# Retention with its norm taken token by token and turned afterwards, and its heads' work placed between projection units

## The chip, the cores and the metric

The kernel runs on one NeuronCore of one Trainium2 chip. The metric is the device time of one execution in microseconds (us).

## The reference, cut to what matters

The network has two conditioned transformer layers, then two post-normed ones; the first of those holds the retention that is changed here. There are 256 tokens and 1024 features.

```python
# x: (B, T, D) = (1, 256, 1024);  H = 4 heads, dk = 256, dv = 512, chunks of C = 128 tokens
proj = x @ w_in                                   # w_in: 1024 x 6144
q, k, v, gate = jnp.split(proj, [1024, 2048, 4096], axis=-1)
q = _rope(q);  k = _rope(k) * dk ** -0.5
def body(state, inp):                             # one chunk of tokens, all heads
    s = einsum('bhid,bhjd->bhij', qi, ki) * intra # decay gamma^(i-j) for i >= j, else 0
    inner = einsum('bhij,bhje->bhie', s, vi)
    cross = einsum('bhid,bhde->bhie', qi * xi, state)
    state = gamma_c * state + einsum('bhjd,bhje->bhde', ki * zeta, vi)
    return state, inner + cross
mu  = mean(y, axis=-1);  var = mean((y - mu) ** 2, axis=-1)     # over the 512 of a head, per token
y   = (y - mu) * rsqrt(var + 1e-5)
mix = (silu(gate) * y) @ w_out                    # w_out: 2048 x 1024
```

With two chunks the recurrence is the same as one causal 256 x 256 score matrix with decay, and both kernels compute it so. After it come `x = layer_norm(alpha * x + mix)` and a SwiGLU.

## The kernel before, in words

**Layout and precision.** Activations lie with features on partitions and tokens along the free dimension (`[128, feature block, 256 tokens]`). Every weight product is done in three fast passes on fp32r operands: each operand is split into a high part (a copy in fp32r) and a low part (the rest), and `product3` (L260) issues hi*hi, hi*lo and lo*hi. Other products (scores, outputs, norms) are plain fp32 matmuls, each of which appears in the trace as two passes. A transpose appears as one.

**Units.** Weights stream in units of 1024 rows x 256 columns (1 MB) through four raw buffers. SyncE issues the DMA of a unit once the unit four before it has been split. `act_split` copies the raw unit to its high part on ScalarE, `dve_split` subtracts on VectorE for the low part; there are three split buffers, so unit n+3 is split only when PE has finished unit n. Both functions look two units ahead of the one they are called for. `pe_pair` does a unit's two blocks of 128 columns (48 matmuls of 256 columns), `project_rows` the same for the values, with tokens on the output's partitions.

**Order.** There is no scheduler: each engine runs its instructions in the order in which its own function writes them, and semaphores count them. `Engine.bank` gives out the eight PSUM banks in rotation and lets PE wait for the consumer of the tile that held the bank eight allocations ago.

**Retention** (`Retention`, L1608; `pe_retention`, `act_retention`, `dve_retention`, `pool_retention`):
- eight units of q and k, each 128-block of which is copied to `rt_raw` by ScalarE and rotated (a product with `rt_rot` on PE, GpSimd and VectorE elementwise);
- eight units of v, two units a head, copied from PSUM to `rt_v` by VectorE;
- eight units of the gate, two units a head, through Silu to `rt_g` on ScalarE;
- then the heads' block, a loop over six steps in which scores run for head i, outputs for head i-1, and mean and norm for head i-2. `pe_ret_scores` gives 128 x 384 scores, VectorE multiplies the decay in (`rt_S`, two buffers). `pe_ret_outputs` gives y with features on partitions, in four blocks of 128 for a head. The mean over features is a product with ones, centred by VectorE; squares by ScalarE, summed by 16 passes with one column (`pe_ret_norm`); the root is on ScalarE, the reciprocal and a diagonal matrix on VectorE, and its product with ones spreads 1/std over the partitions. VectorE multiplies it in, GpSimd multiplies the gate by y (`rt_g`), ScalarE and VectorE split the result into `rt_hi` and `rt_lo`.

`pe_deep_out` then multiplies by `w_out` in eight units: for each 256 output columns one over heads 0 and 1, one over heads 2 and 3. `act_layer_norm` and its partners follow, with a root on ScalarE. The input of the retention is the final norm's result, split by `act_program` and `dve_program` into `k.x`.

Of the kernel before, what the change touches and what calls it, by code (L numbers as in the profile page):

```python
# [1606 lines left out]

class Retention:  # L1608
    def __init__(self, k):
# [13 lines left out]
        self.dst = [(self.q if m < 8 else self.k)[:, m % 8, :] for m in range(16)]  # L1623


RET_COLS = [256 * c for c in range(8)]

# [10 lines left out]
def pe_retention(e, x):  # L1638
    k, w = e.k, e.k.io["ret_w_in"]
    t = Retention(k)  # L1640
    k.after(4, sp_retention)
# [9 lines left out]
    for c in range(8):  # L1651
# [5 lines left out]
        if c == 0:  # L1657
            pe_rope(e, t, "ret", 14, ("raw", "ret", 14))
            pe_rope(e, t, "ret", 15, ("raw", "ret", 15))
    for c in range(8):  # L1660
        u = take(e, ("ret_g", c), w, 0, KC, 4096 + 256 * c, 256)
        pe_pair(e, u, x, T, [("ret_g", 2 * c + j) for j in range(2)], [(k.scalar, ("ret_g", 2 * c + j)) for j in range(2)])
    for i in range(RET_HEADS + 2):
        if i < RET_HEADS:
            pe_ret_scores(e, t, i)
        if i >= 2:
            hd = i - 2
            bank = e.bank(("ret_mean", hd), k.scalar, ("ret_mean", hd))
            for c in range(4):
                e.wait_ge(k.scalar, ("ret_y", hd, c))  # L1670
                mm = e.matmul(bank[:, 0:T], k.ones[:, :], t.y[:, hd % 2, c, :], c == 0, c == 3)
            mm.then_inc(k.product, ("ret_mean", hd))
        if 1 <= i <= RET_HEADS:
            pe_ret_outputs(e, t, i - 1)
        if i >= 2:
            pe_ret_norm(e, t, i - 2)
# [13 lines left out]
def pe_ret_outputs(e, t, hd):  # L1690
    k, s = e.k, hd % 2
    e.wait_ge(k.vector, ("ret_S", hd))
    e.wait_ge(k.vector, ("ret_v", 7, 1))
    for c in range(4):
        e0 = hd * RET_DV + c * P
        bank = e.bank(("ret_o", hd, c), k.scalar, ("ret_y", hd, c))
        e.matmul(bank[:, 0:T], t.v[:, 0, e0:e0 + P], t.S[:, s, 0:T], True, False, loose=True)
        e.matmul(bank[:, P:T], t.v[:, 1, e0:e0 + P], t.S[:, s, T:384], False, True, loose=True).then_inc(
            k.product, ("ret_o", hd, c))


def pe_ret_norm(e, t, hd):
    k = e.k
    bank = e.bank(("ret_stat", hd), k.scalar, ("std", ("ret", hd)))
    e.wait_ge(k.scalar, ("ret_sq", hd, 3))
    for tb in range(TB):
        for c in range(4):
            mm = e.matmul(bank[:, tb:tb + 1], t.sq[:, c, tb * P:(tb + 1) * P], k.ones[:, 0:1], c == 0, c == 3)
    mm.then_inc(k.product, ("ret_stat", hd))
    rows = e.bank(("ret_rows", hd), k.vector, ("ret_normed", hd, 3))  # L1710
    pe_rows(e, TB, [rows[:, tb * P:(tb + 1) * P] for tb in range(TB)])


def act_retention(e):
# [9 lines left out]

    over_tiles(e, "ret", RET_COLS, act_split, lambda i, name: raw(i), lambda e: None)
# [8 lines left out]
    e.wait_ge(k.product, ("ret_g", 15))  # L1734
    for i in range(RET_HEADS + 2):
        if i >= 2:
            hd = i - 2
            e.wait_ge(k.product, ("ret_mean", hd))
            if hd:
                e.wait_ge(k.vector, ("ret_centred", hd - 1, 3))  # L1740
# [684 lines left out]
```

## Time and profile before

| | |
|---|---|
| time, median of 3 runs | 3046.66 us |
| lowest and highest | 3038.80, 3049.42 us |
| the profiled execution's own time | 3043.53 us |
| its span | 3041.7 us |
| TensorE (PE) busy | 2876.0 us, 95% |
| VectorE (DVE) busy | 1336.7 us, 44% |
| ScalarE (ACT) busy | 1022.7 us, 34% |
| GpSimd (POOL) busy | 149.8 us, 5% |
| DMA | 406.20 MB |

How to read it: the span runs from the first to the last instruction of one execution, and the time is a little longer. All times in the views are us from the span's start, durations of single instructions are in us in a timeline and in ns as means. PEld is PE's loading of the stationary operand, which overlaps its matmuls. A matmul's own duration holds its way through the array, so the pace of a row of them is read from start to start. L96 is the helper that issues all matmuls, L99 transposes, L103 and L104 activations (without and with an accumulated sum), L107 two-tensor operations of VectorE and GpSimd. The granted clock of PE is given as a share of full speed, 1.00 for 2.4 GHz and 0.50 for 1.2 GHz.

### The profile page before, as it was taken

To read this page: it belongs to the slowest core of one execution; us is meant where nothing else is said; L and a number is where in the kernel's file an instruction comes from. 1 tells how busy PE (TensorE), PEld (TensorE's weight loads), DVE (VectorE), ACT (ScalarE), POOL (GpSimd) and SP (SyncE) were. 2 spreads that over 40 slices of the span, in tenths; PEclk is the share of its full clock that TensorE was granted. 3 is DMA by queue.
4 is the path that set the end of the run, shared out by engine and by line. 5 is a ranking of instruction groups with operands and counts; after the bars stand their busy time and mean duration, and the time that the engine had idled before them with its cause. 6 is when DMAs were issued, how large, how long until landed. Compare 5 with 4: busy or idle time off the path is not lost.

```text
span 3041.7 us, 41711 instructions
## 1 busy us (share of the span) xinstructions
PE 2876.0 (95%) x18212; PEld 2535.8 (83%) x18212; DVE 1336.7 (44%) x1813; ACT 1022.7 (34%) x1322; POOL 149.8 (5%) x166
## 2 busy tenths in 40 slices
PE   6999999799999999999989799999889989999898
PEld 4878778588787877877878589999889989989898
DVE  3323242364433234323354555564455543546554
ACT  3222232332321223222242443444344444323443
POOL 1000010000000000000011000010110010000100
PEclk9999999968999999999999899999899999959999
DMA  7434354501434434344333045555145545544452
GB/s 236 153 113 152 117 168 130 162 1 51 130 118 146 143 128 146 125 139 146 114 116 127 15 139 181 167 174 186 61 145 187 168 153 183 168 52 93 138 194 80
DMA packets 398181, 406.20 MB, mean 134 GB/s; under 512 B 7216, under 2 KB 397056, under 8 KB 397872
## 3 DMA queue, kind: packets, MB, share of 16 engines
q1 hardware_dynamic: 398000, 403.53, 42.3%
q8 instruction: 145, 2.38, 0.3%
q14 instruction: 36, 0.29, 0.0%
HBM read 402.38 MB, written 1.12 MB: 133 GB/s over the span
## 4 chain that ended last, share of the span: by engine, by line
PE 87%; DVE 6%; ACT 4%; DMA 1%; issue 1%; POOL 1%; SPq 0%; POOLq 0%; ACTq 0%; DVEq 0%
PE bank L96 86%; DVE w_lo L107 1%; PE bank L99 1%; ACT w_hi L103 1%; DVE tmp L115 1%; ACT x_hi L103 1%; POOL acc L107 1%; ACT df_e L104 1%; DVE x_lo L115 0%; DMA w_raw<-in_ffn_w_in 0%; DVE df_e L115 0%; ACT sq L103 0%; DMA w_raw<-in_mix_w_out 0%; DMA hT<-in_hT 0%; DVE df_sc L124 0%
## 5 line engine op out<-in xcount | busy, mean ns | idle before, releaser
L107 DVE TENSOR_TENSOR w_lo<-w_raw,w_hi 128x2048 fp32r<-128x2048 f32 (+2 forms) x331 | 693.4, 2098 | 951.2 <-ACT w_hi L103 951.1
L96 PE MATMUL bank<-x_hi,w_hi 128*128 128x256 f32 (+1 forms) x3128 | 1037.1, 332 | 42.9 <-DVE x_lo L115 25.9
L96 PE MATMUL bank<-x_lo,w_hi 128*128 128x256 f32 (+1 forms) x3128 | 1029.6, 329 | 0.0
L96 PE MATMUL bank<-x_hi,w_lo 128*128 128x256 f32 (+1 forms) x3128 | 1028.7, 329 | 0.0
L103 ACT ACTIVATE w_hi<-w_raw 128x2048 fp32r<-128x2048 f32 (+2 forms) x331 | 578.7, 1751 | 588.8 <-PE bank L96 272.2
L96 PEld LDWEIGHTS bank<-x_hi,w_hi 128*128 128x128 f32 x3128 | 602.6, 193 | 98.9 <-issue 49.4
L96 PEld LDWEIGHTS bank<-x_hi,w_lo 128*128 128x128 f32 x3128 | 602.3, 193 | 50.5
L96 PEld LDWEIGHTS bank<-x_lo,w_hi 128*128 128x128 f32 x3128 | 602.5, 193 | 49.3
L96 PE MATMUL bank<-hid_hi,w_hi 128*128 128x512 f32 (+1 forms) x1056 | 356.9, 338 | 0.0
L96 PE MATMUL bank<-hid_hi,w_lo 128*128 128x512 f32 (+1 forms) x1056 | 355.5, 337 | 0.0
L96 PE MATMUL bank<-hid_lo,w_hi 128*128 128x512 f32 (+1 forms) x1056 | 355.5, 337 | 0.0
L96 PEld LDWEIGHTS bank<-hid_hi,w_lo 128*128 128x128 f32 x1056 | 200.6, 190 | 20.7
L96 PEld LDWEIGHTS bank<-hid_lo,w_hi 128*128 128x128 f32 x1056 | 200.7, 190 | 20.1
L96 PEld LDWEIGHTS bank<-hid_hi,w_hi 128*128 128x128 f32 x1056 | 200.7, 190 | 20.1
L103 ACT ACTIVATE hid_hi<-tmp 128x512 fp32r<-128x512 f32 (+1 forms) x132 | 69.2, 524 | 385.0 <-DVE tmp L107 385.0
L96 PE MATMUL bank<-w_hi,x_hi 128*128 128x256 f32 x544 | 155.2, 285 | 0.0
L103 ACT ACTIVATE sg<-bank 128x512 f32<-128x512 f32 (+1 forms) x144 | 70.0, 486 | 252.2 <-PE bank L96 252.0
L96 PE MATMUL bank<-w_hi,x_lo 128*128 128x256 f32 x544 | 154.1, 283 | 0.0
L96 PE MATMUL bank<-w_lo,x_hi 128*128 128x256 f32 x544 | 154.1, 283 | 0.0
L107 DVE TENSOR_TENSOR tmp<-bank,sg 128x512 f32<-128x512 f32 (+1 forms) x132 | 73.4, 556 | 172.4 <-PE bank L96 172.2
L107 POOL TENSOR_TENSOR acc<-acc,sq 128x512 f32<-128x512 f32 (+1 forms) x49 | 55.2, 1126 | 1596.8 <-ACT sq L103 1594.4
L107 DVE TENSOR_TENSOR hid_lo<-tmp,hid_hi 128x512 fp32r<-128x512 f32 (+1 forms) x132 | 73.8, 559 | 77.9 <-ACT hid_hi L103 77.9
(211 smaller groups left out, 2470.5 us busy)
## 6 DMA issues: line engine op xcount, KB each, us to landing
w_raw<-in_ffn_w_in SPq DMA_DIRECT2D x88, 1024.0 KB, 5.7
w_raw<-in_ada_w SPq DMA_DIRECT2D x72, 1024.0 KB, 9.8
w_raw<-in_ffn_w_up SPq DMA_DIRECT2D x44, 1024.0 KB, 5.2
w_raw<-in_attn_w_in SPq DMA_DIRECT2D x36, 1024.0 KB, 5.1
w_raw<-in_ffn_w_out SPq DMA_DIRECT2D x32, 768.0 KB, 4.9
w_raw<-in_ret_w_in SPq DMA_DIRECT2D x24, 1024.0 KB, 5.4
w_raw<-in_ffn_w_out SPq DMA_DIRECT2D x32, 640.0 KB, 4.4
w_raw<-in_odd_w_in SPq DMA_DIRECT2D x12, 1024.0 KB, 5.3
```

What stands on the lines that cost most here:

```text
L96: return Issued(self.eng and self.eng.matmul(out, lhsT, rhs, start=start, stop=stop, skip_group_check=loose))
L99: return Issued(self.eng and self.eng.transpose(out, in_, self.k.ident[:, :]))
L103: return Issued(self.eng and self.eng.activation(out, in_, func, bias=bias, scale=scale))
L104: return Issued(self.eng and self.eng.activation(out, in_, func, bias=bias, scale=scale, accum_out=accum))
L107: return Issued(self.eng and self.eng.tensor_tensor(out, a, b, op))
L115: return Issued(self.eng and self.eng.scalar_tensor_tensor(out, a, s, b, op0, op1))
```

## The change

1. Outputs are computed with tokens on partitions: the stationary operand is the score block (128 keys x 128 queries), the moving one v's 512 columns, three matmuls a head in place of eight. ScalarE copies them out with an accumulated sum.
2. The norm runs on that layout: -mean from the sum, a Square with the bias -mean and an accumulated sum of squares, root, reciprocal, then one VectorE operation for each 128 tokens that adds -mean and multiplies by 1/std. The products with ones, the diagonals and their product go.
3. `pe_ret_turn` turns the normed y by eight transposes a head. VectorE multiplies the gate by it straight from PSUM, two feature blocks at a time; GpSimd does nothing any more after the rotations. High and low parts are made of two blocks at a time.
4. The heads' block after the projections is gone. Scores of heads 0 to 3 stand behind value units 1 to 4, outputs of heads 0 and 1 behind value units 5 and 7, those of heads 2 and 3 behind gate units 2 and 4, the turns behind gate units 1, 3, 5 and 7. ScalarE and VectorE have their parts at the matching places of their own orders. `rt_S` has four buffers.
5. The final norm's result goes to a smaller operand `x2`, so that scores, y and squares find room beside it while it is still in use.

```diff
+        self.sc = k.place("rt_sc", MID + 55808, [P, RET_HEADS, 4, TB])
-        self.S = k.place("rt_S", XN + 6144, [P, 2, 384])
-        self.y = k.place("rt_y", XN + 9216, [P, 2, 4, T])
-        self.sq = k.place("rt_sq", XN + 17408, [P, 4, T])
+        self.S = k.place("rt_S", XN + 16384, [P, RET_HEADS, 384])
+        self.y = k.place("rt_y", XN + 22528, [P, 2, TB, RET_DV])
+        self.sq = k.place("rt_sq", XN + 30720, [P, RET_DV])
...
+RET_V_WORK = {1: ("scores", 0), 2: ("scores", 1), 3: ("scores", 2), 4: ("scores", 3), 5: ("outputs", 0), 7: ("outputs", 1)}
+RET_G_WORK = {1: ("turn", 0), 2: ("outputs", 2), 3: ("turn", 1), 4: ("outputs", 3), 5: ("turn", 2), 7: ("turn", 3)}
...
 def pe_ret_outputs(e, t, hd):
+    bank = e.bank(("ret_o", hd, 0), k.scalar, ("ret_y", hd, 0))
+    e.matmul(bank[:, :], t.S[:, hd, 0:P], t.v[:, 0, vs], True, True).then_inc(k.product, ("ret_o", hd, 0))
+    bank = e.bank(("ret_o", hd, 1), k.scalar, ("ret_y", hd, 1))
+    e.matmul(bank[:, :], t.S[:, hd, P:T], t.v[:, 0, vs], True, False)
+    e.matmul(bank[:, :], t.S[:, hd, T:384], t.v[:, 1, vs], False, True).then_inc(k.product, ("ret_o", hd, 1))
+def pe_ret_turn(e, t, hd):
+    for i in range(2):
+        bank = e.bank(("ret_t", hd, i), k.vector, ("ret_gated", hd, i))
+        e.wait_ge(k.vector, ("ret_normed", hd, 1))
+        for c in range(2):
+            for tb in range(TB):
+                at = (2 * i + c) * P
+                mm = e.transpose(bank[:, c * T + tb * P:c * T + (tb + 1) * P], t.y[:, hd % 2, tb, at:at + P])
+        mm.then_inc(k.product, ("ret_t", hd, i))
...
 def act_retention(e):
+    def outputs(hd):
+        for tb in range(TB):
+            e.wait_ge(k.product, ("ret_o", hd, tb))
+            e.activation(t.y[:, hd % 2, tb, :], k.out_of(("ret_o", hd, tb))[:, :], ACT.Copy, accum=t.sums(hd, tb)).then_inc(
+    def spreads(hd):
+        e.wait_ge(k.vector, ("ret_mean", hd))
+            e.activation(t.sq[:, :], t.y[:, hd % 2, tb, :], ACT.Square, bias=t.neg_mean(hd, tb),
+                         accum=t.spread(hd, tb)).then_inc(k.scalar, ("ret_sq", hd, tb))
+        e.activation(t.rstd(hd), t.spread(hd), ACT.Sqrt, scale=1.0 / RET_DV, bias=k.eps[:, 1:2]).then_inc(
+    def high(hd):
+            e.wait_ge(k.vector, ("ret_gated", hd, i))
+            e.activation(t.out.hi[:, m:m + 2, :], t.gate[:, m:m + 2, :], ACT.Copy).then_inc(
     for c in range(8):
         act_split(e, ("ret_v", c))
+        if c == 7:
+            outputs(0)
+            spreads(0)
     for c in range(8):
         act_split(e, ("ret_g", c))
+        if c == 1:
+            outputs(1)
+            spreads(1)
         for j in range(2):
             e.wait_ge(k.product, ("ret_g", 2 * c + j))
             e.activation(t.gate[:, 2 * c + j, :], k.out_of(("ret_g", 2 * c + j))[:, 0:T], ACT.Silu).then_inc(
+        if c in (2, 4):
+            outputs(c // 2 + 1)
+            spreads(c // 2 + 1)
+        if c in (1, 3, 5, 7):
+            high(c // 2)
...
 def dve_retention(e):
+    def outputs(hd):
+        e.wait_ge(k.scalar, ("ret_y", hd, 1))
+        e.tensor_scalar(t.neg_mean(hd), t.sums(hd), -1.0 / RET_DV, ALU.mult).then_inc(k.vector, ("ret_mean", hd))
+        e.wait_ge(k.scalar, ("ret_std", hd))
+        e.reciprocal(t.rstd(hd), t.rstd(hd)).then_inc(k.vector, ("ret_rstd", hd))
+            e.tensor_scalar(y, y, t.neg_mean(hd, tb), ALU.add, t.rstd(hd, tb), ALU.mult).then_inc(
+    def gated(hd):
+            e.wait_ge(k.product, ("ret_t", hd, i))
+            e.tensor_tensor(g, g, k.out_of(("ret_t", hd, i))[:, :].rearrange("p (a b) -> p a b", a=2), ALU.mult).then_inc(
+            e.wait_ge(k.scalar, ("ret", "hi", m + 1))
+            e.tensor_tensor(t.out.lo[:, m:m + 2, :], t.gate[:, m:m + 2, :], t.out.hi[:, m:m + 2, :].bitcast(F32),
...
 def pool_retention(e):
-    e.wait_ge(k.scalar, ("ret_g", 15))
-    for hd in range(RET_HEADS):
-        for c in range(4):
-            m = hd * 4 + c
-            e.wait_ge(k.vector, ("ret_normed", hd, c))
-            e.tensor_tensor(t.gate[:, m, :], t.gate[:, m, :], t.y[:, hd % 2, c, :], ALU.mult).then_inc(
```

## Rows read from the trace of the kernel before

**Rows 1.** The page: busy time of the engines, and engines of the last chain.

```profile
PE 2876.0 (95%) x18212; PEld 2535.8 (83%) x18212; DVE 1336.7 (44%) x1813; ACT 1022.7 (34%) x1322; POOL 149.8 (5%) x166
...
PE 87%; DVE 6%; ACT 4%; DMA 1%; issue 1%; POOL 1%; SPq 0%; POOLq 0%; ACTq 0%; DVEq 0%
```

**Rows 2.** Busy time by stretch: the gates' units, then the heads' block.

```profile
core 0: us, PE busy (x) PEld busy (x) DVE busy (x) ACT busy (x) POOL busy (x), PEclk, DMA share, GB/s
...
2088.00:2132.60 44.60, 44.60 (x374) 44.60 (x373) 18.34 (x8) 20.47 (x24) 0.00 (x0) 1.00 0.56 181
2132.60:2181.00 48.40, 39.91 (x212) 35.92 (x210) 21.26 (x56) 19.52 (x54) 9.44 (x12) 0.83 0.07 22
```

**Rows 3.** Timeline (start us, us, engine): weight loads at the block's start; output projection's first.

```profile
2132.63 2.71 PEld L96 LDWEIGHTS bank<-rt_q,rt_k 128*128 128x128 f32 x16
...
2135.26 2.70 PEld L96 LDWEIGHTS bank<-rt_S,rt_v 128*128 128x128 f32 x16
...
2137.88 1.39 PEld L96 LDWEIGHTS bank<-rt_q,rt_k 128*128 128x128 f32 x8
...
2139.19 1.60 PEld L96 LDWEIGHTS bank<-rt_y,ones 128*128 128x128 f32 x8
...
2180.94 0.56 PE L96 MATMUL bank<-rt_hi,w_hi 128*128 128x256 f32 x1
```

**Rows 4.** Chain that ended last, in order of time, head 1's part.

```profile
2159.25 3.16 POOL rt_g L107 x4
2162.41 0.02 issue
```

**Rows 5.** Timeline of PE: four fp32 passes of 512 columns.

```profile
612.28 1.88 PE L96 MATMUL bank<-four_t,gla_zf 128*128 128x512 f32 x4
614.00 2.08 PE L96 MATMUL bank<-four_a,four_d 128*128 128x256 f32 x8
```

**Rows 6.** Timeline of PE: nine transposes, and what follows.

```profile
2776.85 1.20 PE L99 MATMUL bank<-ident,at_e 128*128 128x128 f32 x9
2777.89 2.12 PE L96 MATMUL bank<-at_v,at_pT 128*128 128x64 f32 x18
```

**Rows 7.** Busy time by stretch, columns as in rows 2: output projection.

```profile
2181.00:2184.90 3.90, 3.90 (x20) 3.90 (x19) 2.87 (x7) 1.25 (x3) 3.07 (x4) 0.50 0.02 4
2184.90:2229.00 44.10, 44.08 (x368) 43.87 (x366) 21.73 (x17) 15.64 (x9) 4.92 (x8) 1.00 0.52 168
```

**Rows 8.** Instructions of ScalarE by form (busy us, mean ns | idle before).

```profile
L103 ACT ACTIVATE w_hi<-w_raw 128x2048 fp32r<-128x2048 f32 x234 | 445.5, 1908 | 392.5 <-PE bank L96 164.0 <-DMA w_raw<-in_ffn_w_in 147.7 <-DMA w_raw<-in_even_w_in 47.8
L103 ACT ACTIVATE sg<-bank 128x512 f32<-128x512 f32 x72 | 42.5, 590 | 168.3 <-PE bank L96 168.3
L103 ACT ACT_TABLE_LOAD x28 | 35.9, 1283 | 1.6 <-POOL cs L130 1.1
L103 ACT ACTIVATE sq<-hT 128x512 f32<-128x512 f32 x51 | 31.9, 630 | 109.7 <-DVE hT L115 62.6 <-DVE hT L107 31.8 <-PE bank L96 10.5
L104 ACT ACTIVATION_READ_ACCUMULATOR at_e<-at_e,at_sc 128x1 f32 x32 | 6.0, 187 | 0.0
```

**Rows 9.** Instructions of VectorE by form.

```profile
L107 DVE TENSOR_TENSOR w_lo<-w_raw,w_hi 128x2048 fp32r<-128x2048 f32 x234 | 536.0, 2295 | 677.6 <-ACT w_hi L103 677.4
L107 DVE TENSOR_TENSOR tmp<-bank,sg 128x512 f32<-128x512 f32 x66 | 45.6, 691 | 159.2 <-PE bank L96 159.2
L111 DVE TENSOR_SCALAR df_e<-df_e,df_sc 128x512 f32<-128x512 f32 x12 | 5.8, 480 | 0.0
```

**Rows 10.** Timeline of ScalarE: the root of the first layer norm.

```profile
2238.18 0.47 ACT L103 ACTIVATE acc<-bank,eps 128x256 f32<-128x256 f32 x1 [1.22 <-PE bank L96]
```

**Rows 11.** Busy time by stretch, columns as in rows 2: around attention's transposes.

```profile
2777.00:2780.00 3.00, 3.00 (x27) 2.87 (x26) 2.75 (x6) 1.33 (x3) 0.00 (x0) 1.00 0.89 287
...
2789.00:2792.00 3.00, 1.03 (x9) 1.07 (x10) 1.99 (x6) 0.84 (x3) 0.00 (x0) 1.00 0.00 0
2792.00:2795.00 3.00, 3.00 (x18) 3.00 (x17) 1.59 (x5) 1.24 (x3) 0.00 (x0) 0.58 0.03 5
```

More of the change, by code:

```diff
@@ L1640, in pe_retention @@
     t = Retention(k)
+    work = {"scores": pe_ret_scores, "outputs": pe_ret_outputs, "turn": pe_ret_turn}
     k.after(4, sp_retention)
@@ L1659, in pe_retention @@
             pe_rope(e, t, "ret", 15, ("raw", "ret", 15))
+        if c in RET_V_WORK:
+            kind, hd = RET_V_WORK[c]
+            work[kind](e, t, hd)
     for c in range(8):
@@ L1662, in pe_retention @@
         pe_pair(e, u, x, T, [("ret_g", 2 * c + j) for j in range(2)], [(k.scalar, ("ret_g", 2 * c + j)) for j in range(2)])
[L1663 to L1668, printed above, removed]
-            for c in range(4):
[L1670 to L1676, printed above, removed]
+        if c in RET_G_WORK:
+            kind, hd = RET_G_WORK[c]
+            work[kind](e, t, hd)
 def pe_ret_scores(e, t, hd):
@@ L1690, in pe_ret_outputs @@
 def pe_ret_outputs(e, t, hd):
-    k, s = e.k, hd % 2
+    k = e.k
+    vs = slice(hd * RET_DV, (hd + 1) * RET_DV)
     e.wait_ge(k.vector, ("ret_S", hd))
[L1693 to L1702, printed above, removed]
-    k = e.k
[L1704 to L1711, printed above, removed]
+    e.wait_ge(k.vector, ("ret_v", 2 * hd + 1, 1))
+    bank = e.bank(("ret_o", hd, 0), k.scalar, ("ret_y", hd, 0))
[4 more added lines that the diff above has]
+def pe_ret_turn(e, t, hd):
+    k = e.k
+    for i in range(2):
[6 more added lines that the diff above has]
+        mm.then_inc(k.product, ("ret_t", hd, i))
 def act_retention(e):
@@ L1770, in turn, with scores @@
         dve_rope(e, t, "ret", i, t.dst[i], t.cs[:, 0, i % 2, :], t.cs[:, 1, i % 2, :])
+    def scores(hd):
+        e.wait_ge(k.product, ("ret_s", hd))
+        e.wait_ge(k.load("decay"), "decay")
+        e.tensor_tensor(t.S[:, hd, :], k.out_of(("ret_s", hd))[:, 0:384], t.dec[:, hd, :], ALU.mult).then_inc(
+            k.vector, ("ret_S", hd))
+    def outputs(hd):
[3 more added lines that the diff above has]
+        e.reciprocal(t.rstd(hd), t.rstd(hd)).then_inc(k.vector, ("ret_rstd", hd))
+        e.wait_ge(k.vector, ("ret_rstd", hd))
+        for tb in range(TB):
+            y = t.y[:, hd % 2, tb, :]
+            e.tensor_scalar(y, y, t.neg_mean(hd, tb), ALU.add, t.rstd(hd, tb), ALU.mult).then_inc(
+                k.vector, ("ret_normed", hd, tb))
+    def gated(hd):
+        for i in range(2):
+            m = 4 * hd + 2 * i
+            g = t.gate[:, m:m + 2, :]
+            e.wait_ge(k.product, ("ret_t", hd, i))
+            e.wait_ge(k.scalar, ("ret_g", m + 1))
+            e.tensor_tensor(g, g, k.out_of(("ret_t", hd, i))[:, :].rearrange("p (a b) -> p a b", a=2), ALU.mult).then_inc(
+                k.vector, ("ret_gated", hd, i))
+        for i in range(2):
+            m = 4 * hd + 2 * i
+            e.wait_ge(k.scalar, ("ret", "hi", m + 1))
+            e.tensor_tensor(t.out.lo[:, m:m + 2, :], t.gate[:, m:m + 2, :], t.out.hi[:, m:m + 2, :].bitcast(F32),
+                            ALU.subtract).then_inc(k.vector, ("ret", "lo", m), ("ret", "lo", m + 1))
+    work = {"scores": scores, "outputs": outputs, "turn": gated}
     dve_split(e, ("ret", 0))
@@ L2252, in build @@
         k.ada_rows = k.place("ada_rows", TEMPS + 14336, [P, 2, 256])
+        k.x2 = Operand(None, k.place("x2_hi", XN, [P, KC, T], F32R), k.place("x2_lo", XN + 8192, [P, KC, T], F32R))
         k.x = Operand(None, k.place("x_hi", XN, [P, KC, 2 * T], F32R), k.place("x_lo", XN + 16384, [P, KC, 2 * T], F32R))
```

92 lines of the change are left out of this document (31 added, 61 removed).

## The prediction

> **What bounds the kernel now.** I began with the page. TensorE (PE) is busy 95% of the span and makes up 87% of the chain that ended last; VectorE is at 44% and ScalarE at 34% [rows 1]. So time goes away only where PE's own work goes away, or where PE waits. The table of stretches finds the place: while the gates are projected, and again in the output projection, PE is busy all the time, but from 2132.60 to 2181.00 us, between the two, it is busy 39.91 of 48.40 us, at a mean granted clock of 0.83 and with DMA at 7% [rows 2, 7]. That stretch is the four heads' work, which stands behind the projections as a block of its own. PE's weight loads give its exact ends: the first for the scores starts at 2132.63, the first for the output projection at about 2180.9 [rows 3], 48.3 us. The chain in order of time shows what fills it: PE, then the copy of the mean, the centring, the squares, the root, the reciprocal, the diagonal, PE again, one after the other, and for the second and third head GpSimd's four multiplications of 3.16 us on top [rows 4].
>
> **What is removed.** The whole block of 48.3 us ends. Not all of it was waiting: the mean over features by a product with ones (8 passes of 256 columns a head), the sum of squares (16 passes of one column) and the broadcast of 1/std (4 passes of 128) are PE work that is gone for good. With tokens on partitions ScalarE's accumulator gives both sums, and mean and 1/std are per-partition scalars. GpSimd's 16 multiplications go too.
>
> **What PE gets instead, between the units.** Scores are unchanged: 16 passes for two heads took 2135.26 - 2132.63 = 2.63 us, 8 for one 2139.19 - 2137.88 = 1.31 us [rows 3]. Four heads: 5.2 us.
> Outputs keep their columns: 4 x (256 + 128) = 1536 before, 3 x 512 = 1536 after. Before, a head took 2137.88 - 2135.26 = 2.62 us [rows 3]. For the new shape, four fp32 passes of 512 columns took 614.00 - 612.28 = 1.72 us, 0.43 us each [rows 5]; six of them, 2.58 us. Four heads: 10.3 us, and at most 10.5.
> The turn is new: eight 128x128 transposes a head. Nine of attention's took 2777.89 - 2776.85 = 1.04 us at the full clock [rows 6], so eight take 0.92 us; at half the clock that is 1.85. I take the first, since PE comes from a full unit each time: 3.7 us for four heads, upper bound 7.4.
> Together 5.2 + 10.3 + 3.7 = 19.2 us, so PE's gap shrinks by 48.3 - 19.2 = 29.1 us.
>
> **The clock behind the block.** Output projection starts cold now: 20 matmuls fill 2181.00 to 2184.90 at a granted clock of 0.50, that is 1.2 GHz, after a stretch in which PE had waited repeatedly; then it is 1.00, 2.4 GHz [rows 7]. 368 matmuls in 44.10 us are 0.12 us each, so 20 would take 2.4 us in place of 3.9, and 1.5 us come back. The bounds are 0 (it starts cold all the same) and 1.9 (half of the 3.9, which is all that a doubled clock can give); PE comes straight from a full unit, so I take 1.5.
>
> **Do the waits stay hidden?** The weights of a unit can be split only when PE has finished the unit three before it. A unit has 48 matmuls, 5.76 us at the 0.12 above, so two units, 11.5 us, lie between; the split costs ScalarE 1.91 us and VectorE 2.30 us after it [rows 8, 9]. 7.3 us are spare, and what is queued ahead of a split on either engine eats into them. Per head, ScalarE gets: two copies of 512 from PSUM (0.59 us each by the nearest row), two squares of 512 (0.63), behind each of these four the reading of its accumulator (0.19), two more copies of 512 (0.63) [rows 8], and one root, for which I take the 0.47 of a wider one as upper bound [rows 10]. Since Silu and Sqrt alternate now, there is also a table load before each root but head 0's and before the next Silu, 1.28 us each [rows 8]. Sum: 1.6 + 1.6 + 1.3 + 0.5 + 2.6 = 7.6 us. With two splits (3.8) and four Silu of half the width of the 0.59 row (some 0.4 each, 1.6) that is 13.0 us against 15.0 us of PE (two units 11.5, outputs 2.6, turn 0.9). VectorE gets two scalings of 0.48, and four 512-wide operations of 0.69 [rows 9], some 4 us a head with the small ones.
> The tightest places, walked through in queue order. (a) After gate unit 4: PE ends it, does outputs(3) until +2.6; ScalarE's second copy ends at +3.4, the mean comes back from VectorE at +3.6, squares, load and root until +7.0, only then the split of unit 7 until +8.9, its low part at +11.2. PE wants it at +2.6 + 5.8 + 0.9 + 5.8 = +15.1. Spare 3.9 us. (b) The root waits for VectorE's mean, and VectorE waits for the root; neither waits for a PE step that is not already issued, so the pair costs only hops. (c) Last head: PE turns at +0.9 after gate unit 7, VectorE gates until +2.0, ScalarE's second high part is out at +2.6, the last low part at +3.4; the output projection reads heads 2 and 3 first after a unit over heads 0 and 1, at +0.9 + 5.8 = +6.7. Spare 3.3 us. (d) Banks: eight allocations back, each consumer is at least one unit old. (e) VectorE's score products (0.56 us) stand after the values' copies, while the split behind them waits for ScalarE anyway. DMA issues are the same ones in the same order; their 48 us pause ends, and the load is then that of the neighbouring stages, at a share near 0.5 [rows 2, 7]. So I cost waits at 0; if a cover is gone, a late split costs PE what is over 3.9 us, plus up to 1.5 us of cold clock behind the wait.
> The final norm's operand moves to other addresses, with the same instructions: 0.
> One cost behind it: the table left active is Silu's, so the first layer norm must load Sqrt's. ScalarE idles 1.22 us ahead of that root now [rows 10], and the load takes 1.28: +0.1 us (0 to 1.3).
>
> **A rule against it.** A switch of tables costs 1.28 us, the mean of 28 loads [rows 8], and the change adds six: five more in the retention, one in the layer norm. The Trainium skill (ScalarE: Activation LUTs, "Table sets: the hidden batching unit" and "Rules for kernel authors") asks to group activations by table set, which the change gives up, and says to budget some 2.7 us for each switch (the same page, under "What ACT_TABLE_LOAD costs", also has a measured 1283 ns). By the 2.7, an estimate from that page, ScalarE would need 13.0 + 2.8 = 15.8 us a head against PE's 15.0, and the layer norm 1.4 us more, and the sum would come out some 5 us higher. The trace agrees with 1.28 and not with 2.7.
>
> **The sum.** 29.1 + 1.5 - 0.1 = 30.5 us. The profiled execution took 3043.53 us (span 3041.7, 1.8 around it), giving 3013.0. It lies 3.1 below the median of the runs, 3046.66, from which I take the forecast: 3046.7 - 30.5 = **3016.2 us**.
>
> **Rivals.**
> 1. *Splits come late* (a chain on ScalarE and VectorE takes PE's wait over). For it: the lock-step in (a) and spare of 3.9 us. Against it: each part of the chain has a row of its own kind and shape. If the chain of a head is 6 us longer, PE waits 6 - 3.9 = 2.1 us and restarts cold for 1.5, for each of the three heads whose chains lie among the gates: 3 x 3.6 = 10.8 us. Time 3027.0.
> 2. *The clock falls at the turns.* After attention's last 16 transposes and a wait, PE ran at a mean clock of 0.58 from 2792 to 2795 [rows 11]. A fall as long as the one of 3.9 us costs 1.5 us, and transposes at half clock 0.9 more: four times 2.4 is 9.6 us, time 3025.8. Against it: PE was busy only 1.03 of the 3 us before that fall, so idleness explains it too, and 2777 to 2780, which begins among nine transposes between matmuls, stays at 1.00 [rows 6, 11]. The Trainium skill (TensorE: Matmul & The Clock Gate, "Part 4: PE-mode transpose") says that transposes do not count as PE work for its clock, which is what would make this rival true. The trace leaves that open, since no turn of it was followed by a fall without a wait between.
> 3. *ScalarE becomes the bound, slower than before.* Place: the gates' eight units. To eat 30.5 us, four heads must each cost 7.6 us over PE's 15.0, so it decides from a period of 22.6 us on ScalarE, against the 13.0 worked out; at 24 us it is 4 x 9 = 36 us, time 3016.2 + 36 = 3052. Only hops between ScalarE and VectorE of several us each could do that; the hops in the chain are 0.02 us [rows 4].
> 4. *The block was hidden anyway, no change.* Then something else would have to hold the output projection back. Weights were there long before (DMA at 7%), and the chain runs through the block. Time 3046.7.
>
> **Chances.** Forecast 0.80, rival 1 0.09, rival 2 0.06, rival 3 0.03, rival 4 0.02. Range: bounds of the terms (transposes +3.7, outputs +0.2, clock -0.4 to +1.5, layer norm +1.2) and the spread of the runs, 3038.80 to 3049.42, take the forecast's own case to 3008 to 3023; reaching to rivals 1 and 2 the range is 3008 to 3028. A measurement of this kernel can tell about 0.3%, 9 us, from no change: faster by more 0.94, within it 0.03, slower 0.03.
>
> **What would show it.** Right: no stretch in which PE is not fully busy between the first value unit and the end of the output projection; first output-projection matmul 29 us earlier and at clock 1.00; units 5.76 us apart, plus 1.3, 2.6 or 0.9 where head work stands; seven table loads in the retention where there were two, and one in the layer norm; GpSimd idle from the last rotation to the output projection. Wrong: PE idle "<- DVE w_lo" at gate units 4 to 7 (rival 1), matmuls at half clock after transposes (rival 2), ScalarE above 90% in the gates' stretch (rival 3).

## The result and the profile after

The changed kernel took 3009.49 us (median of 4 runs, 2991.8 to 3015.92), the kernel before beside it 3044.68 (4 runs, 3038.8 to 3049.42): a ratio of 0.9878, 95% interval [0.9851, 0.9906]. That ratio puts it at 3007.5 us, 37 us less where 30.5 were forecast, just under the range's lower end of 3008; the median of the four, 3009.49, is 1.5 us inside. Two more sets of runs gave 0.9873 [0.9846, 0.9901] and 0.9859 [0.9831, 0.9888]. Over everything that was run, 16 runs of the changed kernel have a mean of 3003.5 us (standard error 2.2) and 56 of the kernel before 3043.6 (1.0): 40.1 us less, with a standard error of 2.4.

The page of the changed kernel, against [rows 1]. PE has lost 13 us of busy time and 28 us of span, so 15 us of the profiled difference were PE waiting; GpSimd has lost 12.7 us.

```profile
PE 2862.8 (95%) x18092; PEld 2518.6 (84%) x18092; DVE 1329.0 (44%) x1785; ACT 1027.4 (34%) x1316; POOL 137.1 (5%) x150
...
PE 89%; DVE 5%; ACT 3%; DMA 1%; issue 1%; POOL 1%; SPq 0%; POOLq 0%; ACTq 0%; DVEq 0%
```

Busy time by stretch (columns as in [rows 2]), from the first score weight load to the output projection's first matmul, then the output projection. They answer to [rows 2, 7]: where PE was busy 39.91 of 48.40 us at a clock of 0.83, it now never stops and never leaves 1.00, and the output projection's 3.90 us at 0.50 are gone.

```profile
2067.98:2167.60 99.62, 99.62 (x762) 93.43 (x761) 52.20 (x60) 56.52 (x79) 0.00 (x0) 1.00 0.46 148
2167.60:2214.00 46.40, 46.38 (x387) 46.17 (x385) 23.42 (x19) 16.45 (x10) 4.82 (x7) 1.00 0.57 184
```

The chain in order of time, 2100 to 2130, which answers to [rows 4]: nothing but PE is left in it, and the eight transposes (line 99) are one link.

```profile
2099.98 24.77 PE bank L96 x191
2124.75 0.87 PE bank L99 x8
2125.62 4.43 PE bank L96 x37
```

ScalarE in that stretch by line, against [rows 8]: each term of the period of 13.0 us can be read here. Per head it is 2 copies (1.2), 2 squares (1.4), 4 accumulator readings (0.8), a root (0.3), 2 table loads (2.6), 2 splits (3.8), 4 Silu (1.5) and 2 high parts (1.3), together 12.9.

```profile
L103 ACT ACTIVATE w_hi<-w_raw 128x2048 fp32r<-128x2048 f32 x14 | 26.7, 1906 | 31.7 <-PE bank L96 31.7
L103 ACT ACT_TABLE_LOAD x7 | 9.0, 1283 | 0.1
L104 ACT ACTIVATE rt_sq<-rt_y,rt_sc 128x512 f32<-128x512 f32 x8 | 5.8, 722 | 5.1 <-DVE rt_sc L111 4.9
L103 ACT ACTIVATE rt_g<-bank 128x256 f32<-128x256 f32 x16 | 5.6, 378 | 5.8 <-PE bank L96 5.5
L104 ACT ACTIVATE rt_y<-bank 128x512 f32<-128x512 f32 x8 | 4.7, 592 | 2.2 <-PE bank L96 2.2
L103 ACT ACTIVATE rt_hi<-rt_g 128x512 fp32r<-128x512 f32 x6 | 3.7, 634 | 2.3 <-DVE rt_g L107 2.3
L104 ACT ACTIVATION_READ_ACCUMULATOR rt_y<-bank 128x1 f32 x8 | 1.6, 199 | 0.0
L104 ACT ACTIVATION_READ_ACCUMULATOR rt_sq<-rt_y,rt_sc 128x1 f32 x8 | 1.5, 186 | 0.0
L103 ACT ACTIVATE rt_sc<-rt_sc,eps 128x2 f32<-128x2 f32 x4 | 1.2, 295 | 0.1
```

To find where the 28.1 us of span went, I cut both traces at the same landmarks (first or last weight load of a tile); these figures are differences of such starts. The row of the layer norm ends with the first q that ScalarE copies out for attention. Two stretches are left out: the rotations, 46.9 us in both, and attention's projections, from that copy to the first score load, 199.9 us in both.

| stretch, us | before | after | difference | forecast |
|---|---|---|---|---|
| start to the first rotation | 1999.0 | 2015.1 | +16.1 | 0 |
| last rotation to the output projection's first load | 135.0 | 105.6 | -29.4 | -29.1 |
| output projection, first to last load | 47.4 | 45.7 | -1.7 | -1.5 |
| layer norm and feed-forward | 234.4 | 234.2 | -0.2 | +0.1 |
| attention, first score load to first load of at_hi | 128.3 | 114.1 | -14.2 | 0 |
| the rest behind it | 250.8 | 252.1 | +1.3 | 0 |

Two stretches whose code is unchanged moved by more than 10 us. The first is scatter: its largest part, from the first gla_q copy to GpSimd's first df_q product, took 1144.7 us here, 1131.0 and 1135.2 in two further traces of the changed kernel, 1130.9 to 1145.3 over all 14 traces of kernels with the new arithmetic, and 1132.6 to 1140.8 over the six with the old. The second isn't so easily dismissed, and most experiments ended up being about it.

In attention PE issues 24 score products of head pairs and then waits 6.5 us for ScalarE's exponentials (timeline of PE, changed kernel):

```profile
2647.38 3.85 PE L96 MATMUL bank<-at_k,at_q 64*128 64x256 f32 x24
2657.74 2.18 PE L99 MATMUL bank<-ident,at_e 128*128 128x128 f32 x9 [6.50 <-ACT at_e L104]
```

The row of nine transposes takes 2.18 us behind the wait and 1.20 in [rows 6]: half clock. What then differs is how long PE stays there. By stretch, kernel before:

```profile
2690.60:2730.60 40.00, 40.00 (x158) 36.43 (x157) 16.43 (x38) 9.07 (x24) 0.00 (x0) 0.50 0.35 40
2730.60:2740.60 10.00, 10.00 (x41) 9.11 (x40) 4.11 (x11) 2.27 (x6) 0.00 (x0) 0.50 0.42 41
2740.60:2770.60 30.00, 30.00 (x222) 28.03 (x221) 21.37 (x51) 13.62 (x36) 0.00 (x0) 0.99 0.65 73
```

and the changed kernel:

```profile
2675.40:2690.40 15.00, 15.00 (x63) 13.89 (x62) 5.83 (x15) 4.54 (x12) 0.00 (x0) 0.50 0.44 54
2690.40:2715.40 25.00, 25.00 (x165) 22.99 (x164) 15.96 (x37) 9.08 (x24) 0.00 (x0) 0.89 0.56 59
2715.40:2740.40 25.00, 25.00 (x191) 23.34 (x190) 19.48 (x45) 10.76 (x29) 0.00 (x0) 1.00 0.71 75
```

PE has no idle time in any of these rows, yet it works at 0.50, some 4 matmuls a us where it later does 7.4. The kernel before leaves that level 78 us after its first score load, the changed one about 48.

### The profile page after: what moved, and what is told of

Read it like the earlier page. It is cut to its first block, busy times and chain, and to the rows that moved or that the text cites. A ratio compares the mean times of both kernels' runs of the same rounds, so it can differ in the third digit from the quotient of the medians.

```text
span 3013.6 us, 41425 instructions
## 1 busy us (share of the span) xinstructions
PE 2862.8 (95%) x18092; PEld 2518.6 (84%) x18092; DVE 1329.0 (44%) x1785; ACT 1027.4 (34%) x1316; POOL 137.1 (5%) x150
## 4 chain that ended last, share of the span: by engine, by line
PE 89%; DVE 5%; ACT 3%; DMA 1%; issue 1%; POOL 1%; SPq 0%; POOLq 0%; ACTq 0%; DVEq 0%
PE bank L96 88%; DVE w_lo L107 1%; PE bank L99 1%; ACT w_hi L103 1%; DVE tmp L115 1%; ACT x_hi L103 1%; POOL acc L107 1%; ACT df_e L104 1%; DVE x_lo L115 0%; DMA w_raw<-in_ffn_w_in 0%; DVE df_e L115 0%; DMA hT<-in_hT 0%; DMA w_raw<-in_mix_w_out 0%; ACT sq L103 0%; DVE df_sc L124 0%
```

## Experiments

### The retention's own steps

**block**: the new arithmetic, with the four heads' work in a block behind the gates, so that only the place is undone.

```
-        if c in RET_G_WORK:
-            kind, hd = RET_G_WORK[c]
-            work[kind](e, t, hd)
...
+    for i in range(RET_HEADS + 2):
+        if i < RET_HEADS:
+            work["scores"](e, t, i)
+        if 1 <= i <= RET_HEADS:
+            work["outputs"](e, t, i - 1)
+        if i >= 2:
+            work["turn"](e, t, i - 2)
... (ScalarE's and VectorE's parts likewise, in a loop behind the gates)
```

> The changed arithmetic and layout (token to a partition, accumulated sums, turn), but the heads' work again as one block behind the gates' projection, in a loop of six steps as before. Theory: the stretch from the first score to the output projection is PE's 19.2 us plus the waits of ScalarE's and VectorE's chain, about 5 us for each of the last steps: some 31 us, against 48.3 before. So the layout alone gives about 17 us, the placing between units the other 12, and the output projection starts cold again (1.5). Ratio about 0.9945. Rival (the placing gives all, the layout only removes PE work of 4 us a head that was hidden anyway): the block stays at 40 us or more, ratio 0.997 or higher.

Ratio 0.9904 [0.9869, 0.9938], below the expected 0.9945, because attention took 104.6 us in its trace where the kernel before has 128.3 (see the next part). The block itself came out near what was expected (19.0 and 10.4 us where 17 and 12 were). Last rotation to output projection took 116.0 us, the output projection 46.9: the new arithmetic takes 19.0 us of block away, placing it between the units 10.4 more, and 1.2 of the 1.7 us behind. Where the remaining waits are can be read in its chain (in order of time, 2146 to 2151), a lock-step of ScalarE and VectorE per head:

```profile
2146.62 1.00 DVE rt_y L112 x2
2147.62 0.47 DVE rt_S L107
2148.09 0.09 DVE rt_sc L111
2148.18 0.02 issue
2148.20 0.82 ACT rt_sq L104 x2
2149.02 0.02 issue
2149.05 0.82 ACT rt_sq L104 x2
2149.87 0.02 issue
2149.89 0.30 ACT rt_sc L103
```

So two thirds of the gain in this stretch came from the arithmetic, one third from the place. How the 19.0 us divide among its parts (GpSimd's multiplications, the products with ones, the joining of operations) no run separates.

**scores**: the kernel before with only the scores moved between the value units (the split input of the retention gets addresses of its own for that).

```
+        if 1 <= c <= 4:
+            pe_ret_scores(e, t, c - 1)
... (and VectorE's product with the decay likewise)
```

> The kernel before with one part of the placing alone: only the scores and their decay product stand behind value units 1 to 4 (four score buffers, and the final norm's result in the smaller operand); outputs and norm stay as they were, in their block. Theory (work that moves from a block with waits in it into full stretches gives back only what was not filling a wait): the values' stretch grows by 5.2 us; the block shrinks by 2.6 us for the two scores at its start and by 0 to 2.6 for those that lay between waits; the sum changes by 0 to +2.6 us, ratio 1.000 to 1.001. Rival (the placing is worth its share of PE work wherever it goes): the block shrinks by all of 5.2 and more, ratio 0.998 or lower.

Ratio 0.9998 [0.9977, 1.0018], last rotation to output projection 135.6 us against 135.0. Moving 5.2 us of PE work out of this block gained nothing: its length is set by its chain and not by PE, and the scores filled its waits.

**turns**: the heads' transposes made 1, 2, 4 and 8 times, so up to 64 in a row.

```
-        for c in range(2):
+        for c in [c for _ in range(2 ** hd) for c in range(2)]:
```

> The changed kernel with the transposes of heads 0, 1, 2, 3 issued 1, 2, 4 and 8 times over (the same results written again), so the turns hold 8, 16, 32 and 64 transposes. Theory (transposes are PE work like others for the granted clock, 0.115 us each): the turns take 0.9, 1.8, 3.7 and 7.4 us, 10.1 us more in all, and the granted clock stays at 1.00 through and behind them. Rival (transposes do not count as work for the clock): behind, or within, the turns of 3.7 and 7.4 us the clock falls to 0.5, the transposes there take up to 0.22 us each, and the unit behind starts at 0.21 us a matmul; 15 us more or above.

The stretch grew by 9.7 us for 88 more transposes, 0.110 each. By stretch, the last turn and what follows:

```profile
2157.00:2165.00 8.00, 8.00 (x73) 8.00 (x73) 2.46 (x2) 1.40 (x3) 0.00 (x0) 1.00 0.59 198
2165.00:2185.00 20.00, 20.00 (x171) 20.00 (x169) 9.61 (x8) 6.93 (x5) 1.14 (x2) 1.00 0.36 115
```

and in the timeline of PE, that turn's 64 transposes and the output projection's first matmul:

```profile
2159.83 7.15 PE L99 MATMUL bank<-ident,rt_y 128*128 128x128 f32 x64
2166.73 0.36 PE L96 MATMUL bank<-rt_hi,w_hi 128*128 128x256 f32 x1
```

7 us of nothing but transposes leave the granted clock at 1.00, through them and behind them. Rival 2 is out. By the rule of the Trainium skill that was set beside it (TensorE: Matmul & The Clock Gate, "Part 4: PE-mode transpose") they do not count as PE work for its clock; this trace does not agree, with 64 of them in 7.15 us at a granted clock of 1.00.

**loads3** and **loads1**: three, and one, more pairs of table switches per head behind the root.

```
+        for i in range(3):
+            e.activation(t.sc[:, hd, 4, 0:1], k.eps[:, 1:2], ACT.Silu).then_inc(k.scalar, ("extra", hd, i))
+            e.wait_ge(k.scalar, ("extra", hd, i))
+            e.activation(t.sc[:, hd, 4, 0:1], k.eps[:, 1:2], ACT.Sqrt).then_inc(k.scalar, ("extra2", hd, i))
+            e.wait_ge(k.scalar, ("extra2", hd, i))
```

> The changed kernel with three more pairs of table switches behind each head's root on ScalarE (a Silu and a Sqrt of one element, results not used), some 9.2 us of ScalarE a head. Theory (the head's chain is hidden by 3.9 us of spare, 3.7 as measured in the changed kernel, and what goes beyond it is paid by PE): PE waits for weights behind gate units 4 to 7, 3 to 6 us for each of heads 1 to 3, and restarts cold; first rotation to first output-projection weights grows from 152.5 us by 10 to 20. Rival (the chain is far from the limit): under 3 us more.

> The changed kernel with one more pair of table switches per head behind its root (two table loads of 1.28 us and two one-element activations of 0.20 us: 3.0 us more on ScalarE a head). Theory (the chain has 3.7 us to spare at its tightest place; ScalarE's sum is 12.9 + 3.0 = 15.9 us a head against PE's 15.0, so the spare shrinks by 0.9 us a head): hidden, last rotation to first output-projection load 105.6 to 107 us and no PE wait of more than 0.5 us there. Rival (the spare is not there): PE waits 3 us and restarts cold for each of three heads, 110 to 119 us. With three such pairs that stretch was 136.2 us, which fits a period of 12.9 + 8.9 = 21.8 us against 15.0 in four heads (27 us) and cold restarts.

Both came out worse than expected: the stretch took 136.2 us with three pairs (expected up to 126) and 111.8 with one (up to 107). The latter is where its rival had it (110 to 119), though PE waits long once and not three times. PE's waits in it (us in total, times, longest; "issue" where the profile names no releaser), with three pairs:

```profile
PE bank L96 <- issue: 7.5, 1, 7.5
PE bank L96 <- ACT rt_g L103: 5.8, 1, 5.8
PE bank L96 <- DVE w_lo L107: 5.3, 1, 5.3
PE bank L96 <- ACT rt_y L104: 3.1, 1, 3.1
```

and with one:

```profile
PE bank L96 <- issue: 4.1, 1, 4.1
PE bank L96 <- DVE w_lo L107: 0.2, 1, 0.2
```

The longest wait with one pair, put down to "issue", ends with the low part of gate unit 7. The chain in order of time and VectorE's timeline:

```profile
2155.08 1.92 ACT w_hi L103
2157.00 2.42 issue
2159.42 7.48 PE bank L96 x48
...
2157.03 2.29 DVE L107 TENSOR_TENSOR w_lo<-w_raw,w_hi 128x2048 fp32r<-128x2048 f32 x1 [3.77 <-ACT w_hi L103]
```

The chains of all four heads lie ahead of a gate unit's split in this stretch (head 0's ahead of unit 2's), so the pairs add 4 x 8.9 = 35.6 us and 4 x 3.0 = 11.9 us to ScalarE there. The stretch grew by 30.6 and 6.2 us: 5.0 and 5.7 us were absorbed, once, and all the rest was paid. PE's waits are 21.7 and 4.3 us of that; the other 8.9 and 1.9 us go with a lower granted clock (0.72 to 0.86 in four 12 us stretches with three pairs, 0.79 in one 8 us stretch with one).

So the 3.7 us that are spare at the tightest place (the low part of unit 7 is out at 2154.99 + 2.29 = 2157.28, PE takes it up at 2161.0) are not a reserve per head. With one pair the splits of units 5 and 7 start 2155.08 - 2138.40 = 16.7 us apart, against 2153.05 - 2138.09 = 15.0 in the changed kernel: ScalarE no longer keeps PE's pace of 15.0, and each chain ends some 1.7 us later against PE than the one before it, until the last split is late enough for the long wait. Busy time alone gives 12.9 + 3.0 = 15.9; the other 0.8 us are ScalarE's own waits for VectorE and PE within a head.

### The 9 us beyond the sum

**again** and **third**: the changed kernel, unedited.

> The changed kernel once more, unedited. In its first profile the retention and its output projection (first rotation to the output projection's last weight load) took 198.2 us against 229.3 before, 31.1 us less, while stages that the change does not touch were 16.1 us slower ahead of it and 14.2 us faster in the dilated attention. Theory (the gain is the 30.5 us of the sum, and what lies outside it is the granted clock of untouched stages, by chance of the run): over many runs the ratio comes to 1 - 30.5/3046.7 = 0.990, within 0.988 to 0.992; the retention again takes 198.2 within 0.5 us, and the attention lies anywhere between 114 and 128 us. Rival (the change also speeds up later stages for good, by when they start): the ratio stays near 0.9878, and the attention takes about 114 us again.

> The changed kernel, unedited, once more, to size the gain over all runs. So far its ten runs have a mean of 3004.3 us against 3044.5 of 37 runs of the kernel before, 40.2 us. Theory A (the retention's own gain of 31.3 us is all, the rest is scatter of the stages that run at half clock for a varying time): the new runs lie around 3013, ratio 0.9897. Theory B (the change gains some 9 us more elsewhere): around 3004, ratio 0.9868. In the trace, last rotation to first output-projection load 105.6 us and output projection 45.7 us whatever the total.

Medians 2999.09 and 2998.24 us, ratios 0.9873 and 0.9859. The retention's stretch took 105.6 and the output projection 45.7 us in both, as in the first trace. Attention took 113.9 and 118.9 us. The theory that the sum is all, with a ratio of 0.990, missed both times: the larger gain repeats.

**before2** and **before3**: the kernel before, unedited, for its attention.

> The kernel before, unedited, for a second trace of its attention. Theory A (attention's stretch at half clock is longer in this kernel than in the changed one): first score load to first product load 123 to 135 us. Theory B (its length goes with the run, not with the kernel): anywhere between 104 and 135, as likely under 120 as over. Last rotation to output projection 135, output projection 47.4 us.

> The kernel before once more, for a third trace: as for the second, theory A 123 to 135 us of attention, theory B under 120 as likely as over it. The total should follow attention's length: about 3044 at 128 us, 3030 at 114.

Attention 123.4 and 128.3 us, beside 128.3 in its first trace and 133.2 in that of *scores*; the retention's stretch 134.9 and 135.1. So, as theory A has it, three traces of the kernel before average 126.7 us and three of the changed one 115.6, without an overlap: 11.1 us.

**warm_before** and **warm_after**, each run in two sets: seven fp32 products of 512 columns fill PE's wait at attention's start, in the kernel before and in the changed one.

```
+        if i == 1:
+            bank = e.bank("warm", k.product, "warm")
+            for _ in range(7):
+                mm = e.matmul(bank[:, :], t.q[:, 0, 0:P], t.v[:, 0, 0:512], True, True)
+            mm.then_inc(k.product, "warm")
```

> The kernel before, with one edit in the dilated attention, far behind the change: 7 fp32 matmuls of 512 columns whose results nobody reads fill the 6.3 us in which PE waits there between the scores of head 1 and the turn of head 0 (in the profile of the repeated changed kernel the granted clock falls to 0.50 in that wait and comes back only 40 us later; before: 70 us later). Theory (the attention's length is set by how long it stays at half the clock after that wait, which differs from run to run and has nothing to do with the change): the attention takes about 96 us in place of 128, at a clock of 1.00; ratio to the kernel before 0.990 or lower, and a narrower spread. Rival (something else makes the attention fast or slow): the attention stays between 104 and 133 us.

> The changed kernel with the same filling in the attention. Theory: its attention takes about 96 us too; then this kernel and the kernel before with the filling differ by the retention and its output projection alone, 31.3 us by the traces (29.4 + 1.7 + 0.2), and not by the 40 us by which the unfilled ones differ on average; time about 2984. Rival (the change shortens something later for good): the two filled kernels differ by 38 us or more.

> The kernel before with seven dummy products in the PE wait at attention's start, once more. Expected: attention 96 us from its first score load to its first product load, as in the first run of it; all runs around 3018 us (first six: mean 3018.5). Its difference to the changed kernel with the same filling should be 31.3 us by theory A (the retention alone), about 40 by theory B.

> The changed kernel with the same seven dummy products, once more. Expected: attention 96 us again; all runs around 2988 us (first four: mean 2988.6), below both kernels. Against the filled kernel before: 31.3 us less by theory A, about 40 less by theory B; the first pair gave 29.9, within some 4 us.

Ratios to the kernel before: 0.9919 [0.9893, 0.9946] and 0.9912 [0.9887, 0.9937] for the filled kernel before, 0.9821 [0.9793, 0.9849] and 0.9780 [0.9756, 0.9804] for the filled changed one, which beats both kernels. Timeline of PE in the latter:

```profile
2638.72 6.28 PE L96 MATMUL bank<-at_v,at_q 128*128 128x512 f32 x14
2645.26 1.20 PE L99 MATMUL bank<-ident,at_e 128*128 128x128 f32 x9 [0.26 <-ACT at_e L104]
```

and by stretch from its first score load:

```profile
2634.90:2662.90 28.00, 27.74 (x169) 22.24 (x169) 18.32 (x40) 10.48 (x28) 0.00 (x0) 1.00 0.69 91
2662.90:2716.90 54.00, 54.00 (x401) 50.18 (x400) 40.10 (x92) 22.91 (x62) 0.00 (x0) 1.00 0.72 94
```

With the wait filled the clock never falls in attention, which took 96.0, 95.9 (before) and 95.9, 95.7 us (changed): the difference between the two kernels there is gone. Over all runs, 12 of the one average 3017.7 us and 9 of the other 2982.0, 35.7 apart with a standard error of 3.1. Retention and output projection differ by 31.1 us in both pairs of traces, so this lies midway between theory A (31.3) and the 40.1 of the unfilled pair, and excludes neither: that attention is the whole of the excess is shown by the traces, not by these times. One expectation missed: the filled kernel before spreads no less (standard deviation 6.4 us over 12 runs, 7.1 over 56 unfilled).

**pad31**, a second trace of it (**pad31b**), **pad13** and **pad4**: the changed kernel with 36, 15 or 5 dummy products ahead of the output projection, so that attention starts 31.1, 10.9 or 4.5 us later.

```
+    pt = Retention(k)
+    bank = e.bank("pad", k.product, "pad")
+    for _ in range(36):
+        mm = e.matmul(bank[:, :], pt.S[:, 0, 0:P], pt.v[:, 0, 0:512], True, True)
+    mm.then_inc(k.product, "pad")
```

> The changed kernel with 36 fp32 matmuls of 512 columns (30.8 us of PE work, results not read) ahead of the output projection, so that everything behind starts as late as in the kernel before. Theory A (how long the attention stays at half clock depends on when it starts within the execution): the time is that of the kernel before, 3044 on average, ratio 1.000. Theory B (it is chance whatever the start, and the excess over the sum is sampling): 3004.3 + 30.8 = 3035 on average, ratio 0.997.

> The change with 30.8 us of dummy products ahead of the output projection, once more, so that attention starts when it does in the kernel before. Its first trace had attention at 128.4 us. Theory A1 (when attention starts decides): 123 to 133 again. Theory A2 (the changed retention decides): 114 to 119 as in the unpadded kernel. Theory B (the run decides): either.

> The changed kernel with 15 dummy products ahead of the output projection, some 13 us, so that attention starts 598.5 us behind the last rotation's weight load, as in the kernel with the work as a block (598.6 us, attention 104.5 us twice). Theory A1 (the moment at which attention starts sets how long it stays at half clock): attention 104 to 110 us. Theory A2 (the length grows with the delay, from 114 to 119 at 585 us to 123 to 128 at 616 us): 118 to 124. Theory A3 (the changed retention sets it): 114 to 119.

> The changed kernel with 5 dummy products ahead of the output projection, some 4 us, so that attention starts 589.5 us behind the last rotation's weight load, as in the kernel with one more pair of table loads a head (589.5 us, attention 128.2 us). Theory A1 (the moment of the start sets it): 123 to 133 us. Theory A2 (grows with the delay) or A3 (the changed retention sets it): 114 to 119.

*pad31* had a ratio of 0.9991 [0.9971, 1.0011]. Its stretch grew by 30.7 us, but the mean of 13 runs, 3040.8, is 37.3 us above the changed kernel's 3003.5 (standard error 3.1; theory A had 3044, theory B 3035). A delay of 31 us thus seems to cost 6.6 us more than itself, as the change gains 9 more than itself, here by two standard errors only. Attention took 128.4, 123.5, 123.4 and 123.3 us in the four traces, all longer than the 114 to 119 of the undelayed kernel. That is outside theory A1's 104 to 110 for *pad13* and outside what A2 and A3 had for *pad4*, so none of the three stands as it was put. Stretches of *pad13*:

```profile
2651.80:2701.80 50.00, 49.90 (x195) 45.21 (x196) 22.29 (x48) 13.57 (x37) 0.00 (x0) 0.50 0.40 49
2701.80:2711.80 10.00, 10.00 (x48) 9.10 (x47) 4.09 (x9) 2.29 (x7) 0.00 (x0) 0.58 0.39 40
2711.80:2741.80 30.00, 30.00 (x224) 27.83 (x222) 21.96 (x51) 11.43 (x31) 0.00 (x0) 1.00 0.67 73
```

**block2**: a second trace of *block*, whose first had attention at 104.6 us.

> The new arithmetic as a block behind the gates, once more. Its first trace had attention at 104.6 us and its other nine runs spread from 3004 to 3048. Theory A (the kernel sets the length): 100 to 110 us again. Theory B (the run sets it): elsewhere between 104 and 135. Last rotation to output projection 116, output projection 46.9 us either way.

104.5 us again, and in both traces the half-clock stretch ended 20 to 30 us behind the first score load. Stretches of *block*:

```profile
2668.60:2678.60 10.00, 10.00 (x47) 9.10 (x46) 4.09 (x9) 2.29 (x7) 0.00 (x0) 0.57 0.35 40
2678.60:2740.60 62.00, 62.00 (x462) 57.66 (x462) 45.88 (x105) 25.32 (x68) 0.00 (x0) 1.00 0.73 95
```

The granted clock of every run points the same way. Its missing share times the span, doubled, is the time at half clock: 268.7 us in the mean of 16 runs of the changed kernel (standard error 5.9), 309.9 (2.4) in the 52 of the kernel before that have it listed, 281.0 (4.7) in 13 of the kernel with 36 dummy products. The retention and its output projection account for 20.5 of the 41.2 us between the first two (in the trace of before). If PE is busy in the rest, it costs half of it, by estimate: 10.3 us for the change beyond its own stretch, where 9 were measured, and 6.2 us for the delay beyond itself, where 6.6 were.

All traces whose wait is not filled, by how long after the last rotation attention started:

| kernels | start, us | attention, us |
|---|---|---|
| after, again, third | 585.4 | 114.1, 113.9, 118.9 |
| loads1; pad4 | 589.5; 589.9 | 128.2; 123.3 |
| turns | 593.0 | 123.3 |
| pad13 | 596.3 | 123.4 |
| block, block2 | 598.6, 598.5 | 104.6, 104.5 |
| before, before2, before3 | 616.2 to 616.7 | 128.3, 123.4, 128.3 |
| loads3; pad31, pad31b | 616.1; 616.5 | 123.4; 128.4, 123.5 |
| scores | 616.8 | 133.2 |

The length goes with the kernel to within 5 us, and values lie near steps of 5 (104.5, 114, 119, 123.4, 128.3, 133.2). It isn't a function of the start alone: *pad13* started 2 us from *block* and took 19 us more. Nor is it set by the changed retention alone, since delays of 4 to 31 us behind it lengthened it. The length differs by how long the clock stays at 0.50 after the wait: 20.5 us in *block*, 40.9 in *after*, 71.7 in *before*, 81.8 in *scores*. What sets it stays open.

## Why the prediction was right and wrong

**The block.** -29.1 us forecast, -29.4 measured, in every trace of the changed kernel within 0.1. Its terms hold: the eight transposes take 0.90 us (0.92), the outputs are paced at 0.43 us a pass (weight loads at 2146.61, 2147.03, 2147.46), no unit waits. *block* and *scores* show what the sum only assumed, that the block's length was its chain.

**The clock behind the block.** -1.5 forecast, -1.7 measured.

**Waits at 0.** Right, and the spare at place (a) is 3.7 us where 3.9 was worked out. The squares took 0.72 us, not 0.63, and the root 0.29, not 0.47, which nearly cancel. But rival 1's price used this spare once for each of three heads, 3 x (6 - 3.9 + 1.5) = 10.8. *loads1* and *loads3* show that it is spent once and that all four heads count: 4 x 6 = 24 us more on ScalarE, less the 5 to 6 absorbed, would by estimate have cost 18 to 19 us. The rival didn't happen; its price was too low.

**Layer norm.** The table load stands ahead of the first root, and ScalarE's idle time there fell from 1.22 [rows 10] to 0.18 us. The root still waits for PE, so the load was hidden whole, where 0.1 was forecast.

**The rule against it.** Seven loads in this stretch at 1283 ns; a switch from the last accumulator reading to the root took 2137.88 - 2136.58 = 1.30 us. The trace agrees with the price taken from [rows 8]. It does not agree with the some 2.7 us that the Trainium skill (ScalarE: Activation LUTs, "Rules for kernel authors") budgets for a switch.

**The step that failed** is the sum itself, "3046.7 - 30.5": it set every stage behind the output projection at 0, and no rival had one of them move. The retention gave 31.1 us, and attention, untouched and 430 us later, another 11.1 between the means of three traces each: its clock stayed at 0.50 for 71.7 us before and 40.9 after in the first traces. 42.2 explains the 40.1 of all runs within their error, and filling attention's wait removed the difference in attention. Why that stretch at half clock got shorter stays open. That attention's clock was low for some 70 us stood in the trace of before, in the three rows shown above; [rows 11] begin 36 us behind the end of that stretch and bear only on transposes. This stage, at half clock with PE fully busy, had a length that its work didn't fix (104.5 to 133.2 us in the traces for the same instructions), and its bounds belonged in the range: at the full clock it takes 96 us, so up to 32 us less.

That the first profile's 28.1 us of span lies near the 30.5 forecast is luck: 16.1 us of scatter ahead of the change and 14.2 us of attention nearly cancel in it.

**The range.** Its lower end took the spread of the three runs shown, 3038.8 to 3049.4. Its upper end left that spread out: the bounds there add up to 3016.2 + 3.7 + 0.2 + 1.5 + 1.2 = 3022.8, with the spread to 3025.6 and not 3023, on which nothing hangs, as the range goes to 3028. Over 56 runs the kernel before spreads from 3023.8 to 3065.1, over 16 the changed one from 2991.8 to 3016.1. 3016.2 is 0.1 us above the slowest run of the changed kernel.

## What to carry to other kernels

Cost a moved block by its chain, and see first which engine sets its length: moving PE work out of a chain-bound block gives nothing, replacing the chain's arithmetic gave two thirds here. A spare found by walking a queue once is spent once, not once per iteration, since a helper engine that falls behind carries its lateness into the next iteration. Before setting untouched stages at zero, look for stretches with PE fully busy at half clock: here one shifted by more than the change's own terms were uncertain, and filling the one wait that starts it (here 6.5 us, by seven products whose result nobody reads) was worth 22 us in the changed kernel and 26 in the one before.

## What the runs showed of the hardware

- In a PE wait of 6.3 to 6.6 us the granted clock fell to 0.50 and stayed there for 20.5 us (*block*) to 81.8 us (*scores*), with PE busy from the wait's end on, on products with 64 rows or 64 columns and transposes; it then returned to 1.00 in the same mix. Attention's length repeats for a kernel within 5 us and grew by 4 to 15 us with delays of 4 to 31 us placed 480 us earlier.
- 64 fp32 transposes in a row (7.15 us) kept the clock at 1.00, at 0.110 us each (*turns*).
- A table switch took 1.30 us on ScalarE from one instruction's end to the next one's start; the four accumulator readings of a head 0.19 to 0.20 us each (*after*).
- ScalarE at 56.52 of 99.62 us busy had almost nothing to give: 3.0 us more per head (*loads1*) already made PE wait 4.3 us.
